# Two stages of a one-core float32 network: an S5 setup in a new order, mLSTM gate rows spread by TensorE

## The chip, the cores and the metric

The kernel runs on one core of a Trainium2 chip. The metric is the device time of one execution in microseconds (us), here the median of three runs. All data is float32; the products marked fp32r take rounded float32 operands, and where full precision is wanted an operand is split into a high part and the rest (hi and lo).

## The reference

A layer of one network (S5 mixer, MLP, gated embedding) and then a layer of a second one run over 2048 tokens of 1024 features. Two pieces matter here. The S5 mixer turns its parameters into powers of a complex diagonal matrix and into the input and output factors built from them, after a root-mean-square norm of x. The second layer has a chunked mLSTM with 4 heads of 128 features (shown in chunks of 64 tokens; the kernel takes 128):

```python
b = jnp.cumsum(lfb, axis=-1)
log_d = b[..., :, None] - b[..., None, :] + ib[..., None, :]
log_d = jnp.where(causal, log_d, NEG)
inter = b + m[..., None]
m_t = jnp.maximum(jnp.max(log_d, axis=-1), inter)
d_mat = jnp.exp(log_d - m_t[..., None])
inter_w = jnp.exp(inter - m_t)
s = jnp.einsum('bhtd,bhsd->bhts', qb, kb) * d_mat
num = (jnp.einsum('bhts,bhsd->bhtd', s, vb)
       + inter_w[..., None] * jnp.einsum('bhvk,bhtk->bhtv', C, qb))
den = jnp.sum(s, axis=-1) + inter_w * jnp.einsum('bhk,bhtk->bht', n, qb)
h = num / jnp.maximum(jnp.abs(den), jnp.exp(-m_t))[..., None]
```

Per chunk and head two rows over the tokens t are needed on all 128 partitions: b - m_t (the exponent, before the part that depends on the key s is added) and inter_w (which scales the queries). The mixed output goes through w_out and is added to x.

## The kernel before, in words

The program is a sequence of stages, each a block in which every engine has its own instruction list and waits on semaphores; all engines meet at a stage's end. The stages: constants, S5 setup, S5 states, S5 outputs, the dense part (all large products), attention, mLSTM, and `finish` (w_out).

**S5 setup** (`s5_setup`, L68). ScalarE squares x in 32 steps (`square`, L148) into two buffers `sq`, and TensorE sums each with four products into `pst` (L384); from the sum come `rms` and, on DVE, the scaling of U in two halves (L325, L328). The input factors are made in 16 quarters `q` of two pairs each: POOL makes quarters 0 to 9 (`POOL_Q`, L366 to L375) and DVE quarters 10 to 15 (`inputs`, L261 to L272), each by six products into a buffer of its own, `ab[0]` for POOL and `ab[1]` for DVE. TensorE transposes a quarter (L414) into one of two PSUM banks `psw`, and ScalarE copies it to `Win` (L186). A maker may write its next quarter when its last one has been transposed (`psw_full`). TensorE's list: 32 squares, `taps(0)`, then the quarters in `TURN_ORDER`, with `taps(1)` (L396) before number 20 of 32 pairs. DVE's list: `factors(0)`, `skips`, `inputs(0..2)`, reciprocal, first half of U, `taps(0)`, `factors(1)`, second half of U, `inputs(3..5)`, `taps(1)`; the `taps` are stored to DRAM by SyncE (L135).

**mLSTM** (`mlstm_chunks`, L2114). 16 chunks of 128 tokens. Each engine runs the function `schedule` over the chunks: in step c it does its stages for chunk c + offset, in a written order, which for TensorE is numerators (c), key products and key transposes (c+2), updates (c+1), output transposes (c-3). SyncE loads groups of two chunks, double-buffered, in one queue: `bc`, `ks`, `qr`, `va` of group g, then `oz` of group g-1, then the store of `om` of group g-4. `bc` holds the two gate rows of each head, which attention's start had stored to DRAM (`rows`), broadcast to 128 partitions. DVE adds the mask to `bc` (`am`, L2290), ScalarE takes the exponential with a bias per key (`dm`, L2257), DVE multiplies it into the scores (`sd`, L2296), and POOL multiplies queries by the second row (`qp`, L2231). ScalarE also weights the keys (`kw`, L2264) and makes the norm of the output (L2270 to L2275).

**finish** (`finish`, L2388). 16 tiles of 128 tokens. SyncE loads `m` (the mixed rows), `z` and `x` of a tile, POOL gates (L2444), ScalarE and POOL split in hi and lo (L2437, L2446), TensorE makes 48 products of 512 columns (L2476), DVE adds.

Of the kernel before, what the change touches and what calls it, by code (L numbers as in the profile page):

```python
# [11 lines left out]
P = 128  # L12
# [52 lines left out]
TURN_ORDER = [0, 1, 2, 10, 3, 11, 4, 12, 5, 13, 6, 14, 7, 15, 8, 9]  # L65


def s5_setup(nc, env, d, ctx):  # L68
# [16 lines left out]
    ab = [sb(f"s5_ab{i}", [P, 2, QS, T, H]) for i in range(2)]  # L85
# [3 lines left out]
    zz = sb("s5_zz", [P, NP, H])  # L89
# [22 lines left out]
    with nc.Block() as block:  # L112
# [28 lines left out]
        def _(act):  # L141
# [39 lines left out]
            for n in range(NP):  # L181
                j = TURN_ORDER[n // QS] * QS + n % QS
                if n in (8, 24):
                    taps(n // 16)
                act.wait_ge(psw_full, n + 1)
                act.copy(Win[:, j].rearrange("p a b m -> p (a b) m"), psw[n % 2][:]).then_inc(win_ready, 1)  # L186

        @block.vector
        def _(dve):
# [101 lines left out]
            def inputs(i):  # L291
# [30 lines left out]
            for i in range(3):  # L322
                inputs(i)
# [8 lines left out]
            for i in range(3, len(DVE_Q)):  # L332
                inputs(i)
# [3 lines left out]
        def _(pool):  # L337
# [23 lines left out]
            for i, q in enumerate(POOL_Q):  # L361
# [13 lines left out]
                pool.tensor_tensor(ab[0][:, 1], abt[:, 0], abt[:, 1], ALU.add).then_inc(ab_ready[0], 1)  # L375
# [3 lines left out]
        def _(pe):  # L379
            pe.wait_ge(blk_set, 1)  # L380
            for i in range(32):
# [1732 lines left out]
def mlstm_chunks(nc, env, d, ctx):  # L2114
# [493 lines left out]
```

## Time and profile before

| | us |
|---|---|
| median of 3 runs (3771.35 to 3780.32) | 3776.54 |
| the profiled execution, in all | 3772.95 |
| its span in the profile | 3771.2 |
| TensorE busy | 3408.7 (90%) |
| DVE, POOL, ScalarE busy | 1622.7, 1247.1, 878.0 |
| mean granted TensorE clock, share of full | 0.953 |

In the page PE is TensorE, PEld its weight loads, DVE VectorE, ACT ScalarE, POOL GpSimd and SPq the queue of SyncE; L12 is line 12 of the kernel before. Bracketed text behind a row says how long the engine had been idle before it and what ended that. TensorE's granted clock (PEclk) is a share of 2.4 GHz: 1.00 is 2.4 and 0.50 is 1.2 GHz. The profiled execution's 3772.95 us are its span and 1.75 us around it.

### The profile page before, as it was taken

Reading aid. Unit: us, or ns where it says so; the run is one execution under the profiler, and the core shown is the slowest. Engines: PE = TensorE matmul, PEld = TensorE weight load, DVE = VectorE, ACT = ScalarE, POOL = GpSimd, SP = SyncE. Lnnn points to the kernel's source line nnn. Section 1 sums busy time; section 2 is a strip of 40 time slices with the busy share of each in tenths; the row PEclk is TensorE's granted clock in tenths of the full one; section 3 lists DMA queues with packets and bytes.
Section 4 is the critical chain, followed back from the end, with each engine's and each line's share of the span. In section 5 each row is a group of like instructions: output and inputs, shape, how many; then the busy total and the mean of one; then the engine's idle time right before and its main releaser. Section 6 shows DMA issues by size and latency. Waiting matters only on the chain. (4 is left out here: it accounts for less than half of the span.)

```text
span 3771.2 us, 42304 instructions
## 1 busy us (share of the span) xinstructions
PE 3408.7 (90%) x16849; PEld 2796.5 (74%) x16849; DVE 1622.7 (43%) x1650; ACT 878.0 (23%) x1305; POOL 1247.1 (33%) x710
## 2 busy tenths in 40 slices
PE   5437999999999999999999999999999997965599
PEld 5425878888888778888878888888778785654487
DVE  5586133333333556860143333334557841634311
ACT  4102121111111441112131111112431111753300
POOL 5540224333333532232243333334442230323321
PEclk8669999999999999999999999999999998987799
DMA  2115211111111113234211111111122223239753
GB/s 109 23 25 111 95 50 45 45 50 50 44 50 50 62 34 123 100 102 154 69 39 53 48 50 48 47 50 48 64 75 92 97 95 141 72 93 199 160 144 109
DMA packets 158657, 293.64 MB, mean 78 GB/s; under 512 B 16160, under 2 KB 98336, under 8 KB 157120
## 3 DMA queue, kind: packets, MB, share of 16 engines
q1 hardware_dynamic: 142400, 249.76, 23.1%
q10 hardware_dynamic: 16128, 42.08, 2.9%
q8 instruction: 91, 1.49, 0.2%
q14 instruction: 38, 0.31, 0.0%
HBM read 227.25 MB, written 64.55 MB: 77 GB/s over the span
## 5 line engine op out<-in xcount | busy, mean ns | idle before, releaser
L1398 PE MATMUL ps_job<-AHL,WH 128*128 128x512 f32 x4480 | 1381.6, 390 | 19.9 <-POOL WL L1110 18.4
L1110 POOL TENSOR_TENSOR WL<-WR,WH 128x1024 fp32r<-128x1024 f32 x216 | 524.9, 2430 | 1518.8 <-ACT WH L891 1518.8
L1398 PEld LDWEIGHTS ps_job<-AHL,WH 128*128 128x128 f32 x4480 | 841.5, 188 | 197.4 <-issue 18.7
L1398 PE MATMUL ps_job<-AHL,WL 128*128 128x512 f32 x2240 | 872.1, 389 | 0.0
L891 ACT CAST WH<-WR 128x1024 fp32r<-128x1024 f32 x216 | 227.7, 1055 | 1592.4 <-PE ps_job L1398 1444.9
L1398 PEld LDWEIGHTS ps_job<-AHL,WL 128*128 128x128 f32 x2240 | 421.0, 188 | 87.4
L1281 DVE TENSOR_TENSOR X<-X,ps_job 128x1024 f32<-128x1024 f32 x128 | 156.1, 1220 | 434.9 <-PE ps_job L1398 354.4
L1398 PE MATMUL ps_job<-FH,WH 128*128 128x512 f32 x768 | 298.8, 389 | 0.0
L1398 PE MATMUL ps_job<-FL,WH 128*128 128x512 f32 x768 | 298.8, 389 | 0.0
L1398 PE MATMUL ps_job<-FH,WL 128*128 128x512 f32 x768 | 298.8, 389 | 0.0
L1271 DVE SCALAR_TENSOR_TENSOR SG<-ps_job,RB 128x1024 f32<-128x1024 f32 x64 | 78.4, 1225 | 450.8 <-PE ps_job L1398 430.2
L1275 DVE TENSOR_TENSOR V<-SG 128x1024 f32<-128x1024 f32 x64 | 206.6, 3228 | 2.2
L1335 DVE SCALAR_TENSOR_TENSOR CV<-CU,d_cw,CV 128x1024 f32<-128x1024 f32 x120 | 198.2, 1699 | 0.0
L1201 DVE TENSOR_TENSOR V<-ps_job,SG 128x1024 f32<-128x1024 f32 x32 | 39.1, 1222 | 366.7 <-PE ps_job L1398 349.9
L1140 POOL TENSOR_TENSOR FL<-V,FH 128x1024 fp32r<-128x1024 f32 x64 | 153.2, 2394 | 77.1 <-DVE V L1275 77.1
L1398 PEld LDWEIGHTS ps_job<-FH,WH 128*128 128x128 f32 x768 | 144.2, 188 | 29.9
L1398 PEld LDWEIGHTS ps_job<-FH,WL 128*128 128x128 f32 x768 | 144.2, 188 | 29.9
L1398 PEld LDWEIGHTS ps_job<-FL,WH 128*128 128x128 f32 x768 | 144.2, 188 | 29.9
L1398 PE MATMUL ps_job<-TH,AHL 128*128 128x512 f32 x512 | 157.6, 389 | 0.0
L1123 POOL TENSOR_TENSOR AHL<-Tt,AHL 128x1024 fp32r<-128x1024 f32 x48 | 138.1, 2896 | 23.6 <-DVE Tt L1228 14.8
L1398 PE MATMUL ps_job<-FH,AHL 128*128 128x256 f32 (+1 forms) x512 | 124.9, 336 | 0.0
L597 PE MATMUL s_psy<-s_mt,s_U 128*128 128x256 f32 x128 | 42.2, 412 | 76.8 <-PEq L29 69.9
(393 smaller groups left out, 4886.3 us busy)
## 6 DMA issues: line engine op xcount, KB each, us to landing
WR<-in_wall SPq DMA_DIRECT2D x248, 512.0 KB, 3.6
fm_scratch<-V ACTq DMA_DIRECT2D x32, 512.0 KB
tm_scratch<-V ACTq DMA_DIRECT2D x28, 512.0 KB
s_U<-in_x_group SPq DMA_DIRECT2D x8, 1024.0 KB, 14.6
s_mt<-z_scratch SPq DMA_DIRECT2D x64, 128.0 KB, 5.0
X<-in_x_feat SPq DMA_DIRECT2D x2, 4096.0 KB, 14.6
m_bc<-rows_scratch SPq DMA_DIRECT2D x8, 1024.0 KB, 20.6
m_oz<-tm_scratch SPq DMA_DIRECT2D x8, 1024.0 KB, 11.2
```

What stands on the lines that cost most here:

```text
L597: pe.matmul(o, U[:, 0, 2 * j + g], m, start=True, stop=False)
L891: act.copy(dst, WR[s][:]).then_inc(hi_done, 1)
L1110: pool.tensor_tensor(dst, raw, src.bitcast(F32), ALU.subtract).then_inc(raw_free, 1)
L1123: pool.tensor_tensor(AL[:, k], gained_at(i, k), AH[:, k].bitcast(F32), ALU.subtract).then_inc(al_done, 1)
L1140: pool.tensor_tensor(halves(FL[:, f]), V[f % 2][:], halves(FH[:, f]).bitcast(F32), ALU.subtract).then_inc(fl_done, 1)
L1201: dve.tensor_tensor(V[s][:], ps4[(job + 2 * s + 1) % 4][:], SG[s][:], ALU.mult).then_inc(mix_done, 1)
L1271: dve.scalar_tensor_tensor(SG[f % 2][:], ps4[(JOB_MLP + f) % 4][:], 0.0, halves(RB[:]), ALU.max, ALU.mult).then_inc(relu_done, 1)
L1275: dve.tensor_tensor(V[f % 2][:], SG[f % 2][:], SG[f % 2][:], ALU.mult).then_inc(v_done, 1)
L1281: dve.tensor_tensor(xm, xm, ps4[(JOB_MLP + F_TILES + m) % 4][:], ALU.add).then_inc(xadd, 1)
L1335: step = dve.scalar_tensor_tensor(CV[:, t], xk, c_w[:, t, k:k + 1], CV[:, t], ALU.mult, ALU.add)
L1398: last = pe.matmul(out, l, r, start=(k == 0 and i == 0), stop=(k == k_tiles - 1 and i == 2))
```

## The change

Three parts.

1. **S5 setup.** POOL and DVE have two buffers each for their quarters and wait for the transposes of the quarter before last. A table `FEED` gives TensorE and ScalarE one common order in which squares 12 to 31, turns and taps alternate. DVE makes four quarters instead of three ahead of the reciprocal. `zz` takes the place of `gain`, which is no longer needed then.
2. **mLSTM.** The broadcast load `bc` and DVE's addition of the mask are gone. DVE places the two gate rows (64 partitions: 4 heads by 16 chunks) by head and splits them in hi and lo (`row_hi`, `row_lo`), once. Per chunk TensorE selects the chunk by a product with a column of `of_chunk`, which spreads the row over 128 partitions in the PSUM bank `e_ps`: hi, lo and the mask by `ident_r` for the exponents, later hi and lo for the query weights. ScalarE reads the exponents from there and copies the query weights to `wq`. `s_ps` is now one bank. The orders within a step are new on all engines. The waits that counted from 2 upward by preset semaphores are written out; they wait for the same events.
3. **Loads.** Group 0 of keys, queries and values is loaded chunk by chunk. The first two tiles of `finish` (of `m` the parts made by attention and convolution, `z` and `x`) are loaded within mLSTM, behind the loads that step g = 3 of SyncE's loop issues; `finish` then loads only the mLSTM part of `m` for them.

```diff
 HALF = NP // 2
-TURN_ORDER = [0, 1, 2, 10, 3, 11, 4, 12, 5, 13, 6, 14, 7, 15, 8, 9]
+FEED = [("square", 12, 20), ("turn", 0), ("square", 20, 24), ("turn", 1), ("turn", 10), ("square", 24, 28), ("turn", 11), ("turn", 2),
+        ("square", 28, 32), ("taps", 0), ("turn", 12), ("turn", 3), ("turn", 13), ("turn", 4), ("turn", 5), ("turn", 6), ("turn", 7),
+        ("taps", 1), ("turn", 14), ("turn", 8), ("turn", 15), ("turn", 9)]
+TURN_ORDER = [step[1] for step in FEED if step[0] == "turn"]
...
-    ab = [sb(f"s5_ab{i}", [P, 2, QS, T, H]) for i in range(2)]
+    ab = [[sb(f"s5_ab{i}{k}", [P, 2, QS, T, H]) for k in range(2)] for i in range(2)]
-    zz = sb("s5_zz", [P, NP, H])
+    zz = gain
...
-            for n in range(NP):
-                j = TURN_ORDER[n // QS] * QS + n % QS
-                if n in (8, 24):
-                    taps(n // 16)
-                act.wait_ge(psw_full, n + 1)
-                act.copy(Win[:, j].rearrange("p a b m -> p (a b) m"), psw[n % 2][:]).then_inc(win_ready, 1)
+            def turn(q):
+                for jj in range(QS):
+                    n = turned(q) - QS + jj
+                    act.wait_ge(psw_full, n + 1)
+                    act.copy(Win[:, q * QS + jj].rearrange("p a b m -> p (a b) m"), psw[n % 2][:]).then_inc(win_ready, 1)
...
+            for step, *at in FEED:
+                if step == "square":
+                    for i in range(*at):
+                        square(i)
+                    if at[1] == 32:
+                        inverse()
+                elif step == "turn":
+                    turn(*at)
+                else:
+                    taps(*at)
...
-                if i:
-                    dve.wait_ge(psw_full, turned(DVE_Q[i - 1]))
-                product(ab[1][:, 0], ab[1][:, 1], [bb[:, r, js, None, :] for r in range(2)],
+                if i >= 2:
+                    dve.wait_ge(psw_full, turned(DVE_Q[i - 2]))
+                product(ab[1][i % 2][:, 0], ab[1][i % 2][:, 1], [bb[:, r, js, None, :] for r in range(2)],
...
-            for i in range(3):
+            for i in range(4):
...
-                if i:
-                    pool.wait_ge(psw_full, turned(POOL_Q[i - 1]))
-                then(pool.tensor_tensor(ab[0][:, 0], abt[:, 0], abt[:, 1], ALU.subtract))
+                if i >= 2:
+                    pool.wait_ge(psw_full, turned(POOL_Q[i - 2]))
+                then(pool.tensor_tensor(ab[0][i % 2][:, 0], abt[:, 0], abt[:, 1], ALU.subtract))
...
-            taps(0)
-            done = [0, 0]
-            for n in range(NP):
-                q, jj = TURN_ORDER[n // QS], n % QS
-                if n == 20:
-                    taps(1)
-                if jj == 0:
-                    done[e] += 1
-                    pe.wait_ge(ab_ready[e], done[e])
...
+                i = (POOL_Q, DVE_Q)[e].index(q)
+                pe.wait_ge(ab_ready[e], i + 1)
+                for jj in range(QS):
+                    n = turned(q) - QS + jj
+                    if n >= 2:
+                        pe.wait_ge(win_ready, n - 1)
...
+            for i in range(12):
+                square(i)
+            for step, *at in FEED:
+                if step == "square":
+                    for i in range(*at):
+                        square(i)
+                elif step == "turn":
+                    turn(*at)
+                else:
+                    taps(*at)
...
-    s_ps = [ps(f"m_s_ps{i}", [P, H, MC]) for i in range(2)]
-    kt_ps, x_ps = ps("m_kt_ps", [P, H, P]), ps("m_x_ps", [P, H, P])
+    s_ps, e_ps, kt_ps, x_ps = (ps(f"m_{n}_ps", [P, H, MC]) for n in ("s", "e", "kt", "x"))
...
+            def keys(a, b, s, k_sem, q_sem):
+                src_k, src_q = (d["fm"][M_QK.start + i * H:M_QK.start + (i + 1) * H, :, chunks(a, b)].rearrange("k p n -> p k n") for i in (1, 0))
+                at = slice(a % LG * MC, (a % LG + b - a) * MC)
+                need(sp, kt_done, a - LG)
+                sp.dma_start(ks[:, s, :, at], src_k).then_inc(k_sem, 16)
+                need(sp, qp_done, a - LG)
+                sp.dma_start(qr[:, s, :, at], src_q).then_inc(q_sem, 16)
...
-            transfers = ((0, load_rows), (0, load_keys), (0, load_values), (-1, load_gates), (-4, store))
+            transfers = ((0, load_keys), (0, load_values), (-1, load_gates), (-4, store))
...
+                if g == 3:
+                    for s in range(2):
+                        by_tile = lambda v: v[:, :, s * OT:(s + 1) * OT].rearrange("k p n -> p k n")
+                        sp.dma_start(env["o_m"][:, s, 0:A_TILES], by_tile(d["mixed"][0:A_TILES])).then_inc(env["ld_m"][s], 16)
+                        sp.dma_start(env["o_m"][:, s, N_AM:], by_tile(d["mixed"][N_AM:])).then_inc(env["ld_m"][s], 16)
+                        sp.dma_start(env["o_z"][:, s], by_tile(d["fm"][C_Z])).then_inc(env["ld_m"][s], 16)
+                        sp.dma_start(env["o_x"][:, s], by_tile(d["x2"])).then_inc(env["ld_x"][s], 16)
...
-                pool.wait_ge(bc_ld[grp(c)], landed(c))
...
+                pool.wait_ge(wcp_done, c + 1)
...
-            schedule([(1, queries), (-1, gate_o), (-2, gate_z)])
+            schedule([(-1, gate_o), (-2, gate_z), (1, queries)])
...
+            def row_weights(c, s):
+                act.wait_ge(w_done, c + 1)
+                need(act, qp_done, c - 1)
+                act.copy(wq[:, s], e_ps[:]).then_inc(wcp_done, 1)
...
-            schedule([(2, weighted_keys), (2, weights), (-1, rms)])
+            schedule([(2, weights), (1, row_weights), (2, weighted_keys), (-1, rms)])
...
+            for i, r in enumerate((rows.T, rows.B)):
+                dve.tensor_tensor(by_head[i][:], r[:, None, :].to_broadcast([R, H, MC]), of_head[:, :, None].to_broadcast([R, H, MC]),
+                                  ALU.mult).then_inc(row_set, 1)
+                dve.wait_ge(row_set, 3 * i + 1)
+                dve.tensor_copy(row_hi[i][:], by_head[i][:]).then_inc(row_set, 1)
+                dve.wait_ge(row_set, 3 * i + 2)
+                dve.tensor_tensor(row_lo[i][:], by_head[i][:], row_hi[i][:].bitcast(F32), ALU.subtract).then_inc(row_set, 1)
...
-                dve.tensor_tensor(am[:, s], bc[:, grp(c), 0, :, cols(c)], mask[:, None, :].to_broadcast([P, H, MC]), ALU.add).then_inc(am_done, 1)
...
-            schedule([(1, scores), (0, new_state), (-2, normalise), (0, quotient), (-4, output), (3, exponents)])
+            schedule([(1, scores), (-2, normalise), (0, new_state), (-4, output), (0, quotient)])
...
+            def spread(c, i, stop):
+                at = of_chunk[:, c:c + 1].to_broadcast([R, P])
+                pe.matmul(flat(e_ps[:]), at, flat(row_hi[i][:]), start=True, stop=False)
+                return pe.matmul(flat(e_ps[:]), at, flat(row_lo[i][:]), start=False, stop=stop)
+
+            def exponents(c, s):
+                pe.wait_ge(row_set, 3)
+                pe.wait_ge(of_set, 3)
+                need(pe, dm_done, c)
+                need(pe, wcp_done, c - 1)
+                spread(c, 0, False)
+                pe.matmul(e_ps[:], ident_r[:], mask_r[:, None, :].to_broadcast([P, H, MC]), start=False, stop=True).then_inc(e_done, 1)
+
+            def row_weights(c, s):
+                pe.wait_ge(row_set, 6)
+                pe.wait_ge(dm_done, min(c + 2, N_MC))
+                spread(c, 1, True).then_inc(w_done, 1)
+
...
-            schedule([(0, numerators), (2, key_products), (1, updates), (-3, turn_output)])
+            schedule([(2, exponents), (0, numerators), (1, row_weights), (2, key_products), (1, updates), (-3, turn_output)])
...
+                if c < 2:
+                    sp.dma_start(m[:, s, A_TILES:N_AM], by_tile(d["mixed"][A_TILES:N_AM, :, at])).then_inc(ld_m[s], 16)
+                    return
```

TensorE in the S5 setup, before (`s_pst` are the squares, `s_psw` the turns, `s_psz` the taps):

```order
L384 MATMUL s_pst<-s_sq,s_blk 128x128 x128
L396 MATMUL s_psz<-s_ca,s_ab 64x64 x64
L414 MATMUL s_psw<-ident,s_ab 128x128 x80
L396 MATMUL s_psz<-s_ca,s_ab 64x64 x64
L414 MATMUL s_psw<-ident,s_ab 128x128 x48
```

and with the change:

```order
L396 MATMUL s_pst<-s_sq,s_blk 128x128 x80
L422 MATMUL s_psw<-ident,s_ab 128x128 x8
L396 MATMUL s_pst<-s_sq,s_blk 128x128 x16
L422 MATMUL s_psw<-ident,s_ab 128x128 x16
L396 MATMUL s_pst<-s_sq,s_blk 128x128 x16
L422 MATMUL s_psw<-ident,s_ab 128x128 x16
L396 MATMUL s_pst<-s_sq,s_blk 128x128 x16
L408 MATMUL s_psz<-s_ca,s_ab 64x64 x64
L422 MATMUL s_psw<-ident,s_ab 128x128 x56
L408 MATMUL s_psz<-s_ca,s_ab 64x64 x64
L422 MATMUL s_psw<-ident,s_ab 128x128 x32
```

Five quarters (8 transposes each) now stand ahead of the last squares, and the second taps stand ahead of the last four quarters instead of the last six.

SyncE in mLSTM, the loads of one group before:

```order
L2177 DMA m_bc<-rows_scratch 128x8x256
L2183 DMA m_ks<-fm_scratch 128x4x256
L2186 DMA m_qr<-fm_scratch 128x4x256
L2196 DMA m_va<-tm_scratch 128x4x128 x2
L2202 DMA m_oz<-tm_scratch 128x2x1024
```

and with the change from group 3 to group 4, with the tiles of `finish` between:

```order
L2216 DMA m_ks<-fm_scratch 128x4x256
L2218 DMA m_qr<-fm_scratch 128x4x256
L2222 DMA m_va<-tm_scratch 128x4x128 x2
L2244 DMA m_oz<-tm_scratch 128x2x1024
L2260 DMA o_m<-mixed_scratch 128x2x128
L2261 DMA o_m<-mixed_scratch 128x2x128
L2262 DMA o_z<-fm_scratch 128x2x128
L2263 DMA o_x<-x_scratch 128x8x128
L2260 DMA o_m<-mixed_scratch 128x2x128
L2261 DMA o_m<-mixed_scratch 128x2x128
L2262 DMA o_z<-fm_scratch 128x2x128
L2263 DMA o_x<-x_scratch 128x8x128
```

The 1-MB load at the head of each group is gone, and eight smaller loads stand once in the queue.

TensorE in one step of mLSTM with the change (before, the rows of `m_e_ps` weren't there, and the numerators stood first):

```order
L2399 MATMUL m_e_ps<-m_row_hi,m_of_chunk 128x512
L2400 MATMUL m_e_ps<-m_row_lo,m_of_chunk 128x512
L2408 MATMUL m_e_ps<-m_mask_r,m_ident_r 128x512
L2421 MATMUL m_n_ps<-m_va,m_sd 128x129
L2422 MATMUL m_n_ps<-m_state,m_qp 128x129
...
L2399 MATMUL m_e_ps<-m_row_hi,m_of_chunk 128x512
L2400 MATMUL m_e_ps<-m_row_lo,m_of_chunk 128x512
L2430 MATMUL m_s_ps<-m_qr,m_ks 128x128 x4
L2434 MATMUL m_kt_ps<-ident,m_ks 128x128 x4
L2442 MATMUL m_u_ps<-m_va,m_kw 128x129 x4
```

Five products of 512 columns join each step, in two places.

## Rows read from the trace of the kernel before

**Rows 1.** Windows by stage: busy us of PE, PEld, DVE, ACT, POOL; clock; DMA share, GB/s.

```profile
0.00:154.00 154.00, 71.79 (x640) 64.94 (x640) 90.57 (x124) 50.48 (x95) 73.82 (x76) 0.72 0.21 74
...
3366.00:3563.00 197.00, 95.65 (x640) 91.76 (x640) 79.23 (x194) 65.09 (x289) 61.59 (x50) 0.73 0.80 171
```

**Rows 2.** Waits of 50 to 154 us: us in total, times, longest.

```profile
POOL s_ab L371 <- PE s_psw L414: 46.2, 2, 30.3
...
DVE s_tmp L261 <- PE s_psw L414: 34.3, 4, 26.9
```

**Rows 3.** Timeline of the S5 setup; columns: start us, us, engine, line.

```profile
37.18 1.28 POOL L375 TENSOR_TENSOR s_ab<-s_abt 128x512 f32<-128x512 f32 x1
...
72.79 0.69 DVE L261 TENSOR_TENSOR s_tmp<-s_bb,s_psp 128x512 f32<-128x512 f32 x1 [26.94 <-PE s_psw L414]
...
131.10 1.28 POOL L371 TENSOR_TENSOR s_ab<-s_abt 128x512 f32<-128x512 f32 x1 [30.29 <-PE s_psw L414]
...
152.66 0.59 ACT L186 COPY s_Win<-s_psw 128x512 f32<-128x512 f32 x1 [0.27 <-PE s_psw L414]
...
154.13 3.62 SPq L423 DMA_DIRECT2D s_mt<-z_scratch  x8
```

**Rows 4.** Timeline of the S5 setup, the durations of its parts.

```profile
31.06 20.98 PE L384 MATMUL s_pst<-s_sq,s_blk 128*128 128x128 f32 x160 [4.30 <-ACT s_sq L148]
...
43.11 0.69 DVE L264 TENSOR_TENSOR s_ab<-s_tmp 128x512 f32<-128x512 f32 x1
...
61.91 1.06 POOL L366 TENSOR_TENSOR s_abt<-s_bb,s_pwr 128x512 f32<-128x512 f32 x1
...
68.89 1.05 POOL L366 TENSOR_TENSOR s_abt<-s_bb,s_pwr 128x512 f32<-128x512 f32 x1
...
81.19 1.57 DVE L264 TENSOR_TENSOR s_ab<-s_tmp 128x512 f32<-128x512 f32 x1
...
85.59 1.76 DVE L325 RECIPROCAL s_pst<-s_rms 128x256 f32<-128x256 f32 x1
...
96.99 45.64 SPq L135 DMA_DIRECT2D z_scratch<-s_zs  x16
...
110.29 8.69 DVE L328 TENSOR_TENSOR s_U<-s_U,s_pst 128x8192 f32<-128x8192 f32 x1
...
137.91 0.85 DVE L315 TENSOR_TENSOR s_zs<-s_psz,s_zz 16x256 f32<-16x256 f32 x2
```

**Rows 5.** Windows in the mLSTM stage: its first loads, and a stretch in mid-stage.

```profile
3368.00:3378.00 10.00, 0.00 (x0) 0.00 (x0) 0.00 (x0) 0.00 (x0) 0.00 (x0) 0.50 0.45 85
...
3419.00:3425.00 6.00, 2.83 (x13) 2.86 (x14) 4.72 (x12) 0.00 (x0) 2.83 (x2) 0.50 1.06 338
```

**Rows 6.** DMA issues of the mLSTM stage: count, KB each, median us to landing.

```profile
m_bc<-rows_scratch SPq DMA_DIRECT2D x8, 1024.0 KB, 20.6
```

**Rows 7.** Timeline of mLSTM, the same DVE instruction of two neighbouring chunks.

```profile
3535.94 0.69 DVE L2323 TENSOR_TENSOR m_hz<-m_hm,m_rr 128x512 f32<-128x512 f32 x1
...
3541.33 0.69 DVE L2323 TENSOR_TENSOR m_hz<-m_hm,m_rr 128x512 f32<-128x512 f32 x1
```

**Rows 8.** Window over the same six microseconds.

```profile
3535.00:3541.00 6.00, 5.53 (x48) 5.18 (x47) 4.67 (x14) 4.55 (x22) 4.25 (x4) 1.00 0.29 56
```

**Rows 9.** Timeline: first product of mLSTM, last numerators, last output.

```profile
3385.41 2.05 PE L2344 MATMUL m_s_ps<-m_qr,m_ks 128*128 128x128 f32 x8 [29.16 <-DMA m_qr<-fm_scratch]
...
3544.85 0.64 PE L2357 MATMUL m_n_ps<-m_va,m_sd 128*128 128x129 f32 x2
...
3557.95 0.69 DVE L2328 TENSOR_TENSOR m_om<-m_x_ps,m_gain 128x512 f32<-128x512 f32 x1 [1.27 <-PE m_x_ps L2374]
```

**Rows 10.** The chain of waits that ended last: start us, us, what.

```profile
3563.46 0.36 SPq L2411
...
3563.87 4.24 DMA o_z<-fm_scratch
...
3585.78 11.19 PE o_y_ps L2476 x48
```

More of the change, by code:

```diff
@@ L331, in _ @@
                     factors(1)
-            for i in range(3, len(DVE_Q)):
+            for i in range(4, len(DVE_Q)):
                 inputs(i)
@@ L380, in _, with square @@
             pe.wait_ge(blk_set, 1)
-            for i in range(32):
+            def square(i):
                 pe.wait_ge(sq_done, i + 1)
@@ L2006 @@
 N_AM = KD - C_TILES
+OT = P
+N_OT = SEQ // OT
 class GateRows:
@@ L2114, in mlstm_chunks @@
 def mlstm_chunks(nc, env, d, ctx):
+    for name, shape in (("o_m", [P, 2, KD, OT]), ("o_z", [P, 2, C_TILES, OT]), ("o_x", [P, 2, KD, OT])):
+        env[name] = env["weights"].enter_context(nc.sbuf_tensor(name, shape, F32, side="right"))
+    _, _, lasting = tools(nc, env["weights"])
+    for name in ("ld_m", "ld_x"):
+        env[name] = [lasting(f"o_{name}{s}") for s in range(2)]
     sb, ps, sem = tools(nc, ctx)
     ident, eps, rows = env["ident"], env["eps"], env["rows"]
-    H = M_HEADS
+    H, R = M_HEADS, rows.n
     tok, dec = rows.tok, rows.dec
@@ L2165, in _ @@
         def _(sp):
-            for s in range(2):
-                sp.sem_inc(st[s], 16)
-            sp.dma_start(gain[:], d["ml_gain"]).then_inc(ld_g, 16)
-            tokens = lambda g: slice(g * LG * MC, (g + 1) * LG * MC)
+            chunks = lambda a, b: slice(a * MC, b * MC)
             last_of = lambda g: (g + 1) * LG - 1
-            def load_rows(g, s):
-                if g >= 2:
-                    sp.wait_ge(am_done, last_of(g - 2) + 3)
-                    sp.wait_ge(qp_done, last_of(g - 2) + 3)
-                sp.dma_start(bc[:, s], d["rows"][:, :, tokens(g)].partition_broadcast(P)).then_inc(bc_ld[s], 16)
@@ new lines, in values @@
+            def values(c, semaphore):
+                src = d["tm"][chunks(c, c + 1), 256:256 + M_W].rearrange("p (h n) -> p h n", h=H)
+                sp.dma_start(va[:, grp(c), c % LG, :, 0:P], src).then_inc(semaphore, 16)
+            def load_keys(g, s):
+                if g == 0:
+                    for c in range(LG):
+                        keys(c, c + 1, s, k_ld[0 if c else 2], q_ld[0 if c else 2])
+                        if c == 0:
+                            sp.wait_ge(va_set, 1)
+                        values(c, va_ld[0 if c else 2])
+                else:
+                    keys(g * LG, (g + 1) * LG, s, k_ld[s], q_ld[s])
@@ L2359, in numerators, with key_products @@
                 last.then_inc(num_done, 1)
+            def key_products(c, s):
+                arrived(pe, k_ld, c)
+                arrived(pe, q_ld, c)
+                need(pe, sd_done, c)
+                for h in range(H):
+                    last = pe.matmul(s_ps[:, h], ks[:, grp(c), h, cols(c)], qr[:, grp(c), h, cols(c)], start=True, stop=True)
+                last.then_inc(s_done, 1)
+                need(pe, kw_done, c)
+                for h in range(H):
+                    last = pe.transpose(kt_ps[:, h], ks[:, grp(c), h, cols(c)], ident[:])
+                last.then_inc(kt_done, 1)
             def updates(c, s):
-                pe.wait_ge(va_ld[grp(c)], LG * landed(c))
-                pe.wait_ge(kw_done, c + 3)
+                values_arrived(pe, c)
+                pe.wait_ge(kw_done, c + 1)
                 pe.wait_ge(c_done, c + 1)
```

215 lines of the change are left out of this document (97 added, 118 removed).

## The prediction

> **What bounds the kernel now.** I read the windows by stage first. The S5 setup (0 to 154 us) keeps no engine busier than 91 of 154 us, and the mLSTM stage (3366 to 3563 us) none busier than 96 of 197 us [rows 1]. Both are chains of waits, and the change edits these two and the first transfers of the last stage. The dense work between them isn't touched.
>
> The list of waits in the S5 setup names two stalls [rows 2]: POOL lost 46.2 us in two waits and DVE 34.3 us in four, all for TensorE transposes that free the one buffer that each maker fills (`ab[0]`, `ab[1]`). The timeline shows why [rows 3]. POOL's first quarter is ready at 38.46 us, but TensorE reaches its first `turn` only after 32 squares and `taps(0)`; POOL loses the shorter of its two waits there (46.2 less 30.3), and DVE, behind three quarters of POOL, writes its second quarter at 72.79 us after 26.94 us of idle time. Later TensorE stands before DVE's fourth quarter and `taps(1)`, and POOL waits 30.29 us until 131.10 us. The last copy ends at 153.25 us, and the next stage starts at 154.13 us.
>
> In the mLSTM stage the windows show 85 GB/s while `bc` alone heads SyncE's queue, and 338 GB/s in a later stretch with other loads in it [rows 5]. The eight `bc` transfers of 1024 KB land 20.6 us after their issue (median) [rows 6]. Two equal instructions of neighbouring chunks that have their data stand 5.39 us apart [rows 7]; the stage spends 197/16 = 12.3 us on each chunk.
>
> **S5 setup, part by part.** POOL's quarters start 6.98 us apart when nothing holds them [rows 4]; with DVE now beside them I take 7.2, so the tenth is ready at 38.46 + 9 x 7.2 = 103 us. DVE starts its first quarter at 41.8 us, two products of 0.69 us before its row at 43.11 us. Six products of 0.69 are 4.1 us; beside POOL two of the six grow to 1.57 us [rows 4], 5.9 us at most; I take 4.9, halfway, so four are ready at 61.4 us. The squares: 160 matmul records took 20.98 us from 31.06 us on [rows 4]. Among them now stand five turns, each eight transposes with two ScalarE copies of 0.59 us behind them, after which ScalarE must fill `sq` again. I take 2.5 us for one alone and 3.6 us for each of the two pairs, 9.7 us, and 1.9 us for the square root with its table: 31.1 + 21.0 + 9.7 + 1.9 = 63.7 us. The squares are the later, so DVE idles 2 us. From its reciprocal (85.59) to the end of the second scaling of U (110.29 + 8.69) it needs 33.4 us [rows 4]: 97.1. Two more quarters (9.8) and `taps(1)` (0.9) end at 107.8. The last eight stores of `zs` were issued from 138.8 (137.91 + 0.85) to 142.6 us (96.99 + 45.64) [rows 4]; with 3 us to land and end the stage that is 114.6 us against 154.13: **39.5 us saved**. POOL's quarters (103) and TensorE's `taps(1)` are covered by DVE's chain; with a DVE chain 5 us shorter POOL would be the last. Bounds: quarters of 4.1 us and undisturbed squares give 107.5 (47 saved); squares at TensorE's lower clock, twice 1.05 us each and partly hidden by ScalarE's pace, about 13 us more (27 saved). `zz` in `gain`'s place costs nothing: both are used by DVE alone, in order.
>
> The rows speak against this part too: a product took 1.57 us where POOL's ran beside it and 0.69 us where POOL stood still [rows 4], and the change takes POOL's standstill away. The Trainium skill (SBUF — State Buffer, "SBUF: two separate sides") says that a DVE instruction with two SBUF inputs and a GpSimd one shut each other out for a whole instruction. By that rule every quarter costs 5.9 us and the setup ends about 3 us later, at 118.
>
> **mLSTM, part by part.** Removed: eight 1-MB transfers and 16 additions of the mask on DVE, which isn't the bound (4.67 of 6 us, [rows 8]), so these return nothing. Added per chunk: five fp32r products of 512 columns on TensorE, one 128x512 copy on ScalarE (0.59 us, [rows 3]), and once nine DVE instructions over 64 partitions, 5 us at most beside the first loads. Such a product costs 11.19/48 = 0.233 us [rows 10], five 1.17 us. In the free stretch TensorE was busy 5.53 of 6 us at a granted clock of 1.00 [rows 8]: 4.97 us of a chunk of 5.39, now 6.1 us. ScalarE: 4.55 of 6, so 4.1 us, now 4.7 us and two waits for TensorE. TensorE becomes the bound; with 0.2 us of handshakes (before 5.39 less 4.97, half of it under the longer work) a chunk takes **6.3 us**.
>
> New waits: POOL's `queries` now waits for the copy; behind it stands the next `gate_o`, and TensorE's next numerators wait for it. Copy and product (POOL 4.25 of 6 us in three products a chunk: 1.3 us) are 1.9 us, while TensorE has key products, updates, output transposes and the next exponents before it, over 3 us: no cost. `e_ps` is one bank for both spreads, so TensorE's row weights wait for the exponentials (about 1.3 us); the numerators stand between, about as long.
>
> DMA for two chunks is 3.1 MB, at 338 GB/s 9.3 us, under 12.6: hidden. Group 0 has six loads for four before, each smaller.
>
> Edges: the first product came at 3385.41 us [rows 9], behind 1 MB of `bc`. It now needs two loads of 0.26 MB and the split rows: I take 3370, the first numerators 8 us later as in the order of work before them, 15 periods (94.5), and a drain of 12 us (before 13.8, from 3544.85 to 3558.64, [rows 9]; two of its waits were for the old order on DVE): 3484.5. The stage change takes 4.8 us as before (3558.64 to 3563.46, [rows 9, 10]): 3489.3, **74 us saved**. The prefetch of the last stage's tiles (1.9 MB, 6 to 8 us) stands on SyncE ahead of group 4's keys, which are due some 12 us after their issue; it costs nothing while this cover holds, else up to 8 us once. Bounds: TensorE at 0.9 of its clock with all handshakes, 6.1/0.9 + 0.4 = 7.2 us, 60 saved; 6.0 us, 79.
>
> For `bc` a page has a price far from the trace's: the Trainium skill (DMA: Bandwidth & Descriptors, "Anatomy of one DMA") fits 2.0 us plus the bytes at 436 GB/s, 4.4 us for 1 MB. By it eight of them return about 35 us, not 74; the 10 us at 85 GB/s [rows 5] speak against it.
>
> **Last stage.** Of the first tile only 0.26 MB of `mixed` is still to come. The wait for `o_z` behind a whole tile was 4.24 us [rows 10]; I take half: **2 us saved** (0 to 3). The 16 tiles of 11.2 us run back to back as before.
>
> **Sum**, against the profiled execution (span 3771.2, in all 3772.95 us): 39.5 + 74 + 2 = 115.5, so 3657.5. That execution lies 3.6 us under the median of the three runs (3776.54); I go 1.5 us towards it: **3659**.
>
> **Rivals.**
> - *The queues stay bound by bytes.* The stage moved 171 GB/s x 197 us = 33.7 MB at a DMA share of 0.80 [rows 1]. Less 8.4 MB and plus 1.9 it is 27.2 MB, at that rate 159 us: 38 saved, in all 79.5, 3695. Against it: 338 GB/s in the same queue [rows 5].
> - *TensorE stays at a mixed clock*: 0.73 over the stage [rows 1], 0.50 where it did nothing [rows 5], 1.00 in the free stretch [rows 8]. If short waits hold it at 0.8, a chunk takes 7.6 us, the stage gives 52, and with slowed squares the setup 30: 84, 3690.
> - *The setup gives nothing*, since a fixed order of squares and turns makes one engine wait for another as before: 76, 3698. Against it: in my sums each turn stands at or after the time when its quarter is ready.
> - *Slower*: the spreads run in four passes as fp32 would, on a TensorE at 1.2 GHz. Five cost 1.17 x 4 x 2 = 9.3 us and the old work 9.9: 19.2 us a chunk, where anything over 12.3 loses. 16 x 6.9 = 110 lost, 41.5 won: 3843. Against it: their operands have the type of the products that took 0.233 us.
>
> **Chances.** Forecast 0.66, mixed clock 0.14, bytes 0.11, setup 0.06, slower 0.03. The likeliest case's own range is 3640 (79 + 47 + 3 saved gives 3645) to 3680; taking in the rivals up to 2 in 10 left out, the range ends at 3696. A measurement of this kernel tells 0.2% (7.5 us) from no change; only the last rival is slower: faster 0.96, within 0.2% 0.01, slower 0.03.
>
> **What would show it.** In the setup: POOL's waits for `psw` under 5 us in all, no idle stretch of DVE over 5 us from 42 to 108 us, the next stage at 108 to 119 us. In mLSTM: after the first chunk no DMA wait over 2 us, chunks 6.0 to 6.8 us apart, a clock over 0.9, `e_ps` products 0.23 us apart. Chunks 8 us apart with DMA waits would mean bytes, a clock under 0.85 the second rival; a last stage that begins after 3470 us would make the forecast wrong.

## The result and the profile after

The changed kernel takes **3664.3 us** (median of 4 runs, 3663.3 to 3666.7) against 3776.3 us (median of 4, 3771.4 to 3780.3): a ratio of 0.9706, 95% interval 0.9693 to 0.9718. Its profiled execution took 3664.25 us with a span of 3662.6 us, 108.6 us shorter than the span of before. The forecast was 3659, with a range of 3640 to 3696.

The windows by stage of the changed kernel, columns as in [rows 1]; the third is the middle of the mLSTM stage:

```profile
0.00:115.00 115.00, 64.26 (x642) 58.41 (x644) 95.42 (x125) 49.08 (x95) 78.99 (x78) 0.87 0.28 99
3329.00:3455.00 126.00, 107.74 (x720) 89.18 (x720) 71.02 (x187) 73.03 (x307) 61.56 (x50) 0.92 0.70 215
3350.00:3430.00 80.00, 79.40 (x556) 65.84 (x554) 48.25 (x134) 54.62 (x235) 46.28 (x37) 1.00 0.78 240
```

DVE's 95 us of work in the S5 setup now lie in 115 us, not in 154, and the mLSTM stage has a bound: TensorE is busy 79.4 of 80 us at a granted clock of 1.00. Before, no engine was busy for half of the stage [rows 1].

The S5 setup in the timeline of the changed kernel (start us, us, engine, line):

```profile
40.63 0.69 DVE L273 TENSOR_TENSOR s_tmp<-s_bb,s_psp 128x512 f32<-128x512 f32 x1
...
56.84 0.69 DVE L273 TENSOR_TENSOR s_tmp<-s_bb,s_psp 128x512 f32<-128x512 f32 x1
...
58.16 1.46 DVE L276 TENSOR_TENSOR s_ab<-s_tmp 128x512 f32<-128x512 f32 x1
...
61.07 0.47 ACT L187 ACTIVATE s_rms<-s_pst,eps 128x256 f32<-128x256 f32 x1
...
62.47 1.76 DVE L337 RECIPROCAL s_pst<-s_rms 128x256 f32<-128x256 f32 x1
...
106.89 1.60 POOL L387 TENSOR_TENSOR s_ab<-s_abt 128x512 f32<-128x512 f32 x1
...
107.40 0.85 DVE L327 TENSOR_TENSOR s_zs<-s_psz,s_gain 16x256 f32<-16x256 f32 x2
...
108.33 3.77 SPq L138 DMA_DIRECT2D z_scratch<-s_zs  x8
...
114.87 3.62 SPq L442 DMA_DIRECT2D s_mt<-z_scratch  x8
```

The next stage starts at 114.87 us; in [rows 3] it was 154.13. No wait of POOL or DVE for a turn is left between 42 and 108 us. The largest that TensorE has there is the other way round, for POOL (list of waits of that stretch: us in total, times, longest):

```profile
PE s_psw L422 <- POOL s_ab L387: 19.6, 5, 6.5
```

The mLSTM stage in the timeline: first load, DVE's first product, first numerators, a mask product, the row products and mask product of the next chunk with the numerators behind them, last numerators, last output, first transfer of the next stage:

```profile
3329.65 0.36 SPq L2216 DMA_DIRECT2D m_ks<-fm_scratch  x1
...
3337.98 0.69 DVE L2354 SCALAR_TENSOR_TENSOR m_sd<-m_s_ps,m_dm 128x512 f32<-128x512 f32 x1 [3.67 <-DMA m_gain<-in_ml_gain]
...
3345.23 0.39 PE L2421 MATMUL m_n_ps<-m_va,m_sd 128*128 128x129 f32 x2
...
3388.95 0.50 PE L2408 MATMUL m_e_ps<-m_mask_r,m_ident_r 128*128 128x512 f32 x1
...
3394.66 0.50 PE L2399 MATMUL m_e_ps<-m_row_hi,m_of_chunk 64*128 64x512 f32 x1
3395.00 0.39 PE L2400 MATMUL m_e_ps<-m_row_lo,m_of_chunk 64*128 64x512 f32 x1
3395.32 0.50 PE L2408 MATMUL m_e_ps<-m_mask_r,m_ident_r 128*128 128x512 f32 x1
3395.65 0.38 PE L2421 MATMUL m_n_ps<-m_va,m_sd 128*128 128x129 f32 x2
...
3438.25 0.46 PE L2421 MATMUL m_n_ps<-m_va,m_sd 128*128 128x129 f32 x2 [0.23 <-DVE m_hb L2386]
...
3449.55 0.69 DVE L2373 TENSOR_TENSOR m_om<-m_x_ps,m_gain 128x512 f32<-128x512 f32 x1 [1.27 <-PE m_x_ps L2449]
...
3455.07 1.10 SPq L2477 DMA_DIRECT2D o_m<-mixed_scratch  x2
```

The stage took 125.4 us (3455.07 less 3329.65) where it took 197.4 (3366.07 to 3563.46). A chunk in full swing takes 6.37 us (3395.32 less 3388.95). The other profiled executions with the same mLSTM code took 125.9 us (experiment 9) and 127.5 and 127.7 (experiments 2 and 3), so some 2 us of such a stage are the execution's. The keys, which once landed 20.3 us after their issue, now land in 7.9 (DMA issues of the stage: KB each, median us to landing):

```profile
m_ks<-fm_scratch SPq DMA_DIRECT2D x7, 512.0 KB, 7.9
```

The last stage, timeline:

```profile
3455.10 1.94 PE L2537 MATMUL o_x_ps<-ident,o_x 128*128 128x128 f32 x8 [5.58 <-PEq L29]
...
3462.48 0.80 PE L2544 MATMUL o_y_ps<-o_wh,o_mh 128*128 128x512 f32 x1 [5.44 <-POOL o_ml L2514]
...
3466.06 0.63 PE L2544 MATMUL o_y_ps<-o_wl,o_mh 128*128 128x512 f32 x1
...
3466.76 0.40 PE L2544 MATMUL o_y_ps<-o_wh,o_ml 128*128 128x512 f32 x1
```

The first `w_out` product stands 7.4 us behind the stage's start, 9.0 us before the change (3572.46 less 3563.46). But products show 0.63 us, TensorE at the lower clock (granted 0.50), for 4.0 us, where they did for 2.2 before. Before, the eight transposes of x (3570.23 to 3572.20) stood right ahead of the first product; now TensorE stood idle for 5.44 us between them and it. The stage takes 207.5 us against 207.7: of the 1.6 us won, 0.8 go back by the last product, and 0.6 behind it, where 6.19 us follow instead of 5.60. Those 0.6 are not the early loads' doing: experiment 9, without them, has 6.13.

So the 108.6 us come from three places and one goes back: 39.3 in the setup, 72.0 in mLSTM, 0.2 in the last stage, less 2.9 in between. The last is taken up below.

### The profile page after: what moved, and what is told of

Read it like the earlier page. It is cut to its first block and busy times, and to the rows that moved or that the text cites. A ratio compares the mean times of both kernels' runs of the same rounds, so it can differ in the third digit from the quotient of the medians.

```text
span 3662.6 us, 42523 instructions
## 1 busy us (share of the span) xinstructions
PE 3414.0 (93%) x16929; PEld 2789.7 (76%) x16929; DVE 1618.2 (44%) x1643; ACT 883.3 (24%) x1323; POOL 1252.3 (34%) x710
```

## Experiments

Each was run beside the kernel before, whose median was 3777.0 us beside experiments 1, 2, 4 and 7, and 3774.9 beside the others. The intervals of the ratios are about 0.0015 to either side, 6 us (experiment 6, with two runs, 0.003), so small differences are read from the stages in the traces.

**1. The S5 part alone.** `s5_setup`, `FEED` and `TURN_ORDER` of the changed kernel in the kernel before.

> Only the S5 part of the change, the mLSTM and last stages as before. Theory (the two parts are separate chains): the stage after the S5 setup begins at 115 us, 39 us earlier, and the program is 36 to 40 us shorter than before: 3737 to 3741 us. In the changed kernel about 3 us of the 39 were lost again between 115 and 333 us, where TensorE's granted clock rose later; if that loss belongs to the shifted start it appears here too (36 to 37), if not the full 39 remain. Rival (the parts lean on each other, for instance through the clock): under 30 us saved.

Measured: 3735.8 us, ratio 0.9893 (0.9877 to 0.9910), 41 us saved; by the spans (3771.2 and 3733.0) 38.2. The next stage starts at 115.66 us. The rest, 71.4 us from here to 3664.3, is what the mLSTM part gave with the setup's in place: the two parts add up.

**2. Two buffers, the old order.**

```diff
-FEED = [("square", 12, 20), ("turn", 0), ("square", 20, 24), ("turn", 1), ("turn", 10), ...
+OLD = [0, 1, 2, 10, 3, 11, 4, 12, 5, 13, 6, 14, 7, 15, 8, 9]
+FEED = [("square", 12, 32), ("taps", 0)] + [("turn", q) for q in OLD[:5]] + [("taps", 1)] + [("turn", q) for q in OLD[5:]]
```

(DVE again makes three quarters before its reciprocal.)

> The changed kernel with its two buffers a maker, but TensorE's and ScalarE's old order (all squares, taps(0), five turns, taps(1), the rest). Theory (both halves are needed): turns after taps(1) wait for the second scaling of U, until about 90 us, POOL then has four quarters of 7.9 us left: the next stage begins near 124 us, 9 us later than in the changed kernel, 3673 us in all. Rival 1 (buffers alone do it): within 3 us of 3664. Rival 2 (the order does it): 20 us or more over 3664.

Measured: 3683.8 us (0.9755, 0.9738 to 0.9771), the next stage at 134.56 us. Its timeline, TensorE's first turn and `taps(1)`, and POOL's longest wait:

```profile
54.91 1.09 PE L421 MATMUL s_psw<-ident,s_ab 128*128 128x128 f32 x8
...
94.63 5.56 PE L407 MATMUL s_psz<-s_ca,s_ab 64*64 64x64 f32 x128 [24.40 <-DVE s_ca L282]
...
103.10 1.27 POOL L382 TENSOR_TENSOR s_ab<-s_abt 128x512 f32<-128x512 f32 x1 [17.96 <-PE s_psw L421]
```

The place was right and the size wrong: TensorE stands 24.4 us before `taps(1)`, and POOL finds both buffers full for 18 us. I had counted from 90 us; turns go on at 100, and DVE itself stood 13.7 us for its third quarter, so its scalings came later too. 19.7 us later, not 9: of the two rivals this is nearly the second (3683.8 less 3664.3 is 19.5 us, the rival wanted 20).

**3. The new order, one buffer.** `i >= 2`, `turned(...[i - 2])` and `ab[..][i % 2]` become `i >= 1`, `[i - 1]` and `ab[..][0]` on POOL, DVE and TensorE.

> The changed kernel with the new order but one buffer a maker. Theory (both halves are needed): a maker has 2.2 us of work before it must write the buffer again, a turn takes 2.8 us at least and stands behind four squares of 1 us in places; each of POOL's quarters grows by 1 to 2 us, the next stage begins at 123 to 135 us, the program takes 3672 to 3684 us. Rival (the order alone does it): within 3 us of 3664.

Measured: 3672.3 us (0.9727, 0.9712 to 0.9742), the next stage at 123.86 us. Its list of waits from 30 to 123 us:

```profile
DVE s_tmp L273 <- PE s_psw L422: 12.2, 4, 6.7
...
POOL s_ab L383 <- PE s_psw L422: 11.8, 4, 6.6
```

Time and start both lie at the lower edge of what was expected. So of the setup's 39.3 us the order alone (with DVE's four quarters ahead of its reciprocal) gives 30.3, the buffers alone 19.6, both 39.3. The two overlap, and the order is the larger part.

**4. The same bytes without the broadcast.** Kernel before:

```diff
-sp.dma_start(bc[:, s], d["rows"][:, :, tokens(g)].partition_broadcast(P)).then_inc(bc_ld[s], 16)
+sp.dma_start(bc[:, s], d["fm"][M_QK.start:M_QK.start + 2 * H, :, tokens(g)].rearrange("(a k) p n -> p a k n", a=2)).then_inc(bc_ld[s], 16)
```

> The kernel before, but each of its eight 1-MB transfers of gate rows is replaced by a plain one of the same bytes and the same 1-KB pieces, each piece read once instead of 128 times (the weights that come of it are other numbers; the mask addition is a min and an addition in one DVE instruction). Theory (the broadcast form of the transfer is what is slow): chunks fall from 12.3 us to 5.5 to 6.5, the program to 3675 to 3700 us. Rival (the queue is bound by bytes): no more than 10 us saved, over 3766.

Measured: 3693.4 us (0.9781, 0.9764 to 0.9797), 83.6 us saved. Its rows: the DMA issues, the waits of mid-stage, and a window that ends before the first `bc` has landed (5.4 us after its issue at 3368.29).

```profile
m_bc<-fm_scratch SPq DMA_DIRECT2D x8, 1024.0 KB, 10.0
...
DVE m_am L2290 <- DMA m_bc<-fm_scratch: 0.7, 2, 0.4
...
3370.00:3373.00 3.00, 0.00 (x0) 0.00 (x0) 0.00 (x0) 0.00 (x0) 0.00 (x0) 0.50 1.00 327
```

In the kernel before, the same wait of the same line:

```profile
DVE m_am L2290 <- DMA m_bc<-rows_scratch: 59.6, 7, 10.3
```

Only the addresses read and DVE's mask instruction have changed, and a queue that ran at 85 GB/s [rows 5], its first `bc` landing after 15.6 us, runs at 327. The stage takes 115.4 us (3367.89 to 3483.29), 10 us less than in the changed kernel, whose TensorE has five products more. The rival that the stage is bound by bytes falls: it moves the same 33.7 MB.

**5. The broadcast in eight pieces**, `for i in range(2 * H)` around transfers of one row kind and head each, and **6. the same with each piece read only eight times**: its source is `fm[M_QK.start + i, 0:16, tokens(g)]` with every partition repeated eight times.

> The kernel before with each broadcast transfer of 1 MB cut into eight of 128 KB, one for each kind of row and head: same bytes, same 1-KB pieces, each still read 128 times. Theory (reading one address 128 times is slow): 3770 to 3780 us, the queue at about 85 GB/s while they run. Rival (one long transfer is what is slow, for instance since its issue holds the queue): 30 us or more faster.

> The same eight transfers of 128 KB, but each reads 16 different partitions' pieces eight times each (other numbers, and the mask addition a min and an addition, as in the plain-load run). Theory, graded (the cost goes with how often a piece is read again): between the plain load's 3693 and 3776 us. If only a piece shared by all 128 partitions is slow: 3690 to 3700. If any repeated piece is as slow: 3770 or more.

Measured: 3774.3 us (0.9998, 0.9987 to 1.0009) and 3711.1 us (0.9831, 0.9802 to 0.9859). One window of each over `bc` transfers, first the 128-fold, then the eightfold:

```profile
3390.00:3396.00 6.00, 5.43 (x41) 5.00 (x39) 0.69 (x1) 4.48 (x16) 0.39 (x1) 0.91 0.97 70
```

```profile
3390.00:3396.00 6.00, 5.54 (x48) 5.37 (x48) 4.12 (x14) 2.30 (x8) 1.27 (x1) 1.00 1.10 322
```

The second window holds other loads besides the last of the `bc` transfers. Where its first ones have the queue to themselves, it runs at 200:

```profile
3372.00:3376.00 4.00, 0.00 (x0) 0.00 (x0) 0.00 (x0) 0.00 (x0) 0.00 (x0) 0.50 0.68 200
```

In the same place the 128-fold pieces ran at 81 (3370 to 3380 us). So the length of the transfer doesn't matter, and of two kernels with the same eight transfers the one that reads a piece eight times is fast. In the first window the DMA engines are busy 97% of the time and move 70 GB/s: it isn't idle engines that make it slow there. What the eightfold reads lose to the plain load (18 us by the medians, the one here of only two runs, 3706.8 and 3715.4; 12.3 us by the mLSTM stage, 127.7 against 115.4) may be the repeats or the 56 transfers more, which this pair doesn't separate. One rival stands untested: both fast forms read `fm`, both slow ones `rows`. No run reads `rows` without repeats, or `fm` with 128, so that the repeats are the cause, and not the tensor, is argued and not shown.

**7. Two products more a chunk.** `spread(c, 0, True)` ahead of `spread(c, 0, False)`.

> The changed kernel with the two row products before the exponents done twice, 32 products more of 512 columns. Theory (TensorE bounds the mLSTM stage, at 0.233 us a product): 16 x 2 x 0.233 = 7.5 us slower, 3671.8 us, chunks 6.7 us apart. Rival (waits between engines or ScalarE set the pace): under 2 us slower. If the products cost what their rows of 0.39 to 0.50 us say: 14 us slower.

**8. fp32 products.** `by_head`, `in_chunk`, `ident` and `mask` in place of their fp32r halves and copies.

> The changed kernel with the rows and the mask multiplied as fp32, three products a chunk in place of five fp32r ones. Theory (fp32 takes four times as long, and TensorE is the bound): 3 x 4 x 0.233 = 2.8 us against 1.17, 1.63 x 16 = 26 us slower, 3690 us. Rival (an fp32 product costs no more than an fp32r one): 2 x 0.233 x 16 = 7.5 us faster, 3657 us.

Measured: 3672.3 us (0.9725, 0.9709 to 0.9742) and 3687.1 us (0.9769, 0.9754 to 0.9784). The mask product of two neighbouring chunks, timeline of the first kernel and of the second:

```profile
3393.53 0.50 PE L2409 MATMUL m_e_ps<-m_mask_r,m_ident_r 128*128 128x512 f32 x1
...
3400.37 0.50 PE L2409 MATMUL m_e_ps<-m_mask_r,m_ident_r 128*128 128x512 f32 x1
```

```profile
3392.19 1.12 PE L2407 MATMUL m_e_ps<-m_mask,ident 128*128 128x512 f32 x2
...
3399.99 1.12 PE L2407 MATMUL m_e_ps<-m_mask,ident 128*128 128x512 f32 x2
```

6.84 us against 6.37: two products more cost 0.47 us, 0.235 each, though a record shows 0.38 to 0.50. TensorE is the bound, and for products added beside their like the price taken from [rows 10] was right.

The five of the change cost more than that. In the timeline of the changed kernel each of them holds the next instruction's start 0.31 to 0.34 us behind its own (hi, lo, mask, numerators at 3394.66, 3395.00, 3395.32, 3395.65; the two of the query weights likewise), 1.64 us for the five from start to start and not 1.17. Only the two added in experiment 7 stand 0.22 to 0.23 apart. Three fp32 products give 7.80 us a chunk, 22.8 us in all and not 26. From start to start they take 3.07 us, 1.02 each; the difference to 1.64 is the 1.43 us measured. Counting the five at 0.233 would make it (7.80 - 6.37 + 5 x 0.233) / 3 = 0.86. So an fp32 product costs 3.1 to 3.7 times an fp32r one here (I had said 4). The 22.8 us are what fp32r is worth here: for the rows, which had to be split for it, and for the mask, which had not.

**9. No prefetch.** The eight early loads removed; `finish` loads its first two tiles whole.

> The changed kernel, but the first two tiles of the last stage are loaded whole in that stage, as before the change. By the forecast's term: 2 us slower (0 to 3). By the trace of the changed kernel, where the first w_out product stood 7.4 us behind the stage's start (9.0 before) but ran at the lower clock for 4.0 us (2.2 before): 0 to 1 us slower. Rival (the transfers ahead of group 4's keys cost the mLSTM stage something): faster than 3664 by 2 us or more.

Measured: 3664.25 us (0.9708, 0.9694 to 0.9723), no difference. Mask products stand 6.37 us apart in both kernels from 3370 us to the last, with one step of 6.7 just before in each, so the early loads cost mLSTM nothing; its first `w_out` product comes 9.0 us after the stage's start (3454.26 to 3463.22) and reaches the full clock 2.2 us later, as before the change. Its last stage takes 208.1 us, 0.6 more than with the early loads. Of the 1.6 us that these win at the first product, 0.7 are left at the last; the clock takes the rest. That is too little to show in the medians.

**10. Three edits more.** The main one:

```diff
-dve.tensor_copy(row_hi[i][:], by_head[i][:]).then_inc(row_set, 1)
+dve.tensor_copy(row_hl[i][0:R], by_head[i][:]).then_inc(row_set, 1)
...
-dve.tensor_tensor(row_lo[i][:], by_head[i][:], row_hi[i][:].bitcast(F32), ALU.subtract).then_inc(row_set, 1)
+dve.tensor_tensor(row_hl[i][R:2 * R], by_head[i][:], row_hl[i][0:R].bitcast(F32), ALU.subtract).then_inc(row_set, 1)
...
-pe.matmul(flat(e_ps[:]), at, flat(row_hi[i][:]), start=True, stop=False)
-return pe.matmul(flat(e_ps[:]), at, flat(row_lo[i][:]), start=False, stop=stop)
+return pe.matmul(flat(e_ps[:]), at, flat(row_hl[i][:]), start=True, stop=stop)
```

> The changed kernel with three edits: the two halves of a gate row lie one above the other on 128 partitions, so that one product spreads them (three products a chunk, not five); DVE waits for the gain only before the first output; in the last stage TensorE turns both tiles of x and does seven unused products while the first w_out product waits, so that its clock is up. Theory: 16 x 2 x 0.233 = 7.5 us, 1.5 us and 2 us: 3653 us. Rival (another engine or a wait sets a chunk at 6.2 us): under 4 us saved.

Measured: **3651.8 us** (median of 5), ratio 0.9675 (0.9662 to 0.9688), 12.5 us under the changed kernel. By the profiles 8.7 of them are the mLSTM stage's (116.7 against 125.4) and 2.4 the last stage's; the other 1.4 lie in stages that are the same in both. Timeline: a chunk, and the start of the last stage.

```profile
3393.30 0.39 PE L2409 MATMUL m_e_ps<-m_mask_r,m_ident_r 128*128 128x512 f32 x1
3393.53 0.38 PE L2422 MATMUL m_n_ps<-m_va,m_sd 128*128 128x129 f32 x2
...
3395.97 0.47 PE L2401 MATMUL m_e_ps<-m_row_hl,m_of_chunk 128*128 128x512 f32 x1 [0.49 <-ACT m_dm L2305]
...
3399.17 0.39 PE L2409 MATMUL m_e_ps<-m_mask_r,m_ident_r 128*128 128x512 f32 x1
...
3448.27 2.83 PE L2547 MATMUL o_y_ps<-o_wh 128*128 128x512 f32 x7
...
3452.72 0.50 PE L2555 MATMUL o_y_ps<-o_wh,o_mh 128*128 128x512 f32 x1 [1.62 <-POOL o_ml L2515]
```

A chunk takes 5.87 us, and in it TensorE now waits 0.49 us for ScalarE's exponentials. So its own work fell by 1.0 us (6.37 to 5.38) with two products fewer, twice their price of 0.47; the wait takes the other half back. The products over 64 partitions are gone, and the numerators begin 0.23 us behind the mask product, no longer 0.33; that this is why is not shown. With `e_ps` as two banks the wait might go; no run tries it.

The first numerators stand 14.1 us behind the stage's start (15.6 in the changed kernel, 17.3 and 17.4 in experiments 2 and 3, which have its mLSTM code), and the last stage takes 205.2 us (207.5): its first product comes 7.8 us behind the stage's start, no sooner, but runs at the full clock. This version beats both kernels.

**The 2.9 us between.** From the start of the stage after the setup to the fifth store of `y_hi` it was 180.1 us before the change. In the changed kernel it is 183.9 (298.78 less 114.87):

```profile
298.78 0.34 SPq L600 DMA_DIRECT2D y_hi_scratch<-s_later  x1
```

In nine of the ten experiments it is 179.7 to 181.2, with the new S5 setup in seven of them. In experiment 6, whose code up to mLSTM is that of the kernel before, it is 184.0. Windows show where this one execution lost it. Two stretches of the changed kernel, and then the like places of the one before:

```profile
212.00:216.00 4.00, 1.47 (x5) 1.32 (x6) 2.99 (x5) 1.28 (x1) 0.00 (x0) 0.50 0.12 29
216.00:220.00 4.00, 4.00 (x15) 2.69 (x15) 3.93 (x4) 0.00 (x0) 0.00 (x0) 0.50 1.13 136
...
252.00:256.00 4.00, 1.22 (x3) 1.04 (x4) 4.00 (x9) 0.85 (x2) 0.00 (x0) 0.83 0.32 41
256.00:260.00 4.00, 4.00 (x21) 3.14 (x20) 3.93 (x4) 0.00 (x0) 0.00 (x0) 0.74 0.94 227
```

```profile
253.00:257.00 4.00, 3.00 (x10) 2.44 (x12) 2.99 (x4) 1.28 (x1) 0.00 (x0) 0.52 0.55 92
257.00:261.00 4.00, 4.00 (x26) 2.97 (x27) 3.93 (x4) 0.42 (x1) 0.00 (x0) 1.00 1.16 131
...
288.00:292.00 4.00, 1.82 (x16) 1.59 (x15) 2.97 (x7) 2.83 (x6) 0.00 (x0) 1.00 0.92 110
292.00:296.00 4.00, 3.19 (x19) 2.54 (x20) 3.97 (x7) 0.00 (x0) 0.00 (x0) 1.00 0.45 139
```

In the changed kernel the clock stood at 0.50 until 220 us, 5.5 us after the first products of the stretch, before the change only some 3 us; and after the next pause (TensorE idle for 2.94 us in the one, 2.98 in the other) it fell again in the one, where it stayed at 1.00 in the other. Experiment 6 lost its 4 us in the same two places. So the loss belongs to the execution, not to the change.

## Why the prediction was right or wrong

The forecast's 3659 lies 5 us under the result, inside its range. The mechanisms held; what was off were sizes, and some were off against each other. Of 115.5 us forecast 108.6 came: the mLSTM stage gave 2.2 less, the last stage 1.8 less, and 2.9 went between the stages, for which the forecast had no term. The 1.5 us towards the median took back part of that.

- **S5 setup: 39.5 us forecast, 39.3 measured**, by errors that cancel. The squares with their turns were done sooner, the square root at 61.5 and not 63.7 us. DVE's quarters take 5.4 us ((56.84 - 40.63) / 3) and not 4.9, so DVE's fourth quarter was the later one and the idle 2 us didn't appear. POOL's quarters take 7.9 us ((108.49 - 37.30) / 9) and not 7.2: "POOL's quarters (103) are covered by DVE's chain" was wrong, both end within 0.3 us of each other. I had charged DVE for the company of POOL, but POOL too little for that of DVE. By the Trainium skill (SBUF — State Buffer, "SBUF: two separate sides") the two shut each other out for a whole instruction where DVE has two SBUF inputs. The rows bear the rule out for the two of DVE's six instructions that read `tmp` twice: 1.46 us in six of the first eight of them (0.74 where one ran undisturbed), while those with one operand in PSUM (`psp`) keep their 0.69. But it isn't every quarter at its 5.9 us, and the setup ended at 114.9, not at 118; and POOL paid too, with products of 1.60 and 1.97 us where it has 1.27 undisturbed.
- **The place of the stalls, the order and the buffers**: right, by experiments 2 and 3. No wait of POOL for `psw`, no idle stretch of DVE over 5 us.
- **mLSTM: 74 us forecast, 72.0 measured.** The term that was mis-sized is "I take 3370, the first numerators 8 us later": 12 us from the stage's start, measured 15.6 (3345.23 less 3329.65). The first product came after 3.2 us (3.9 forecast), but DVE's first product stood 3.7 us idle, about the last 1.6 of them for `gain` alone (the scores' products end at 3336.4 us), which DVE needs much later, and TensorE ran part of the way at the lower clock. With that wait moved and fewer products (experiment 10) the numerators came 1.4 us sooner; which of the two did it isn't separated. The 15 periods took 93.0 us, not 94.5: 6.37 in full swing (6.3 forecast), but 5.95 while there are no outputs to turn yet. That 6.3 came out is partly luck: it was 6.1 us of products and 0.2 of handshakes, and the trace shows TensorE with no idle time at all and the products dearer by about as much (experiments 7 and 8). The drain was 12.0 us (12) and the stage change 4.8 (4.8). Group 0 had five loads before, not four; nothing rests on it.
- **TensorE as the bound**: right, by experiment 7. The removed additions and the added copy are off the path. **0.233 us a product** is what two more cost; the five added took 1.64 us from start to start and not 1.17, which is why the sign "0.23 apart" failed.
- **`bc` slow by its form, not its bytes**: right, by experiments 4 to 6 (whether the repeats or the tensor read make it slow stays open), and the rival at 3695 falls. The rule of the Trainium skill (DMA: Bandwidth & Descriptors, "Anatomy of one DMA"), 2.0 us plus the bytes at 436 GB/s, would have given back 35 us; the plain transfer of experiment 4 returned 84. The page gives that fit for transfers that GpSimd issues, which these, issued by SyncE, are not; the prediction left that out. The plain first megabyte landed 5.4 us after its issue, the broadcast one 15.6, so the fit is no price for a source that 128 partitions share.
- **Mixed clock**: fell, 1.00 from 3350 to 3430 us, 0.92 over the stage. (15 periods of 7.6 us instead of 6.3 leave 55 of the 74 us; the prediction has 52 without saying where the other 3 go.)
- **The slower rival**: fell. Even true fp32 products cost 0.86 to 1.02 us at the full clock, and a chunk with three of them takes 7.80 us, well under 12.3.
- **Last stage: 2 us forecast, 0.2 measured.** The mis-sized term is "I take half" of the 4.24 us wait, without asking what an earlier start does to the clock. The product came 1.6 us earlier; 0.8 went back in 4.0 us at the lower clock, and 0.6 behind the last product, which the kernel without early loads loses as well. Against that kernel the early loads gave 0.6.
- **The prefetch costs nothing**: right (experiment 9).
- "I go 1.5 us towards it": the profiled execution of the changed kernel lies on its median, so the 3.6 us by which the one of before was under its median were not there; with the full 3.6 the same terms give 3661.

## What to carry to other kernels

Where two makers feed one consumer that runs a written order, look first at where in that order it frees their buffers: the order alone gave 30 of 39 us, the second buffers alone 20. Look at a transfer's GB/s while it is alone at the head of its queue; if it is far under the others', test the same bytes from other addresses (and the same addresses in another tensor, which is missing here) before calling the queue bound by bytes. And once TensorE is the bound, contraction rows that stand empty are free: two halves of a split operand, one above the other, take one product instead of two (6.37 to 5.87 us a chunk).

## What the runs showed of the hardware

- A source shared by all 128 partitions (1-KB pieces read 128 times) came at 70 to 85 GB/s with the DMA engines busy up to 97% of the time. The same bytes in pieces read once came at 327, in pieces read eight times at 200 with the queue to themselves; these two read another tensor.
- Two fp32r products of 512 columns over 64 partitions, added beside two like them, cost 0.235 us of TensorE each, though their records show 0.38 to 0.50. Next to products over 128 partitions they and the mask product began 0.31 to 0.34 us apart. An fp32 one cost 0.86 to 1.02.
- The same pause in TensorE's work (2.94 and 2.98 us) brought its clock down in one execution and not in another; with a slower rise before it, 4 us of a kernel's time. And products that follow 5.44 us of idle time ran longer at the lower clock (4.0 us) than products right behind eight transposes (2.2), which took back half of the 1.6 us won by an earlier load. With both tiles of x turned and seven unused products in that pause the stage was 2.4 us shorter.
